# Moving one small matmul ahead of head 0's running sums in TensorE's queue

## The reference

```python
def second_block(x, ...):
    h = rms_norm(x, norm1_g)
    proj = h @ w_in
    q, k, v, glu_a, glu_b = jnp.split(proj, splits, axis=-1)
    q = rms_norm(q.reshape(bsz, seq, 8, 64), q_norm_g)     # per head
    k = rms_norm(k.reshape(bsz, seq, 8, 64), k_norm_g)
    attn = stick_breaking_attention(q, k, v)
    c = glu_a * jax.nn.sigmoid(glu_b)
    c = causal_depthwise_conv(c, conv_dw_w, conv_dw_b)     # 31 taps
    c = jax.nn.silu(layer_norm(c, conv_ln_g, conv_ln_b))
    x = x + jnp.concatenate([attn, c], axis=-1) @ w_out
    ...
# in stick_breaking_attention, per head, s < t:
#   z = q_t.k_s / sqrt(64)
#   weights = exp(log_sigmoid(z) + sum over s<j<t of log_sigmoid(-z_tj))
#   out = weights @ v
```

## Time and profile before

| what | value |
|---|---|
| three timed runs | 1307.55, 1308.39, 1308.89 us; median 1308.39 |
| the profiled execution's own time | 1306.23 us |
| its span, first to last instruction | 1304.5 us |
| mean granted TensorE clock | 0.986 of full |
| busy: TensorE, VectorE, ScalarE, GpSimd | 1258.5, 635.6, 485.4, 530.0 us |

### The profile page before, as it was taken

How to read it: one execution, slowest core, us unless ns; L and a number is a source line. 1 busy time by engine, 2 the same in 40 slices (tenths; PEclk the granted TensorE clock), 3 DMA queues, 4 the chain that set the end, 5 groups by cost and what they waited for, 6 DMA issues and landing times.

```text
span 1304.5 us, 16116 instructions
## 1 busy us (share of the span) xinstructions
PE 1258.5 (96%) x5574; PEld 1018.4 (78%) x5574; DVE 635.6 (49%) x882; ACT 485.4 (37%) x630; POOL 530.0 (41%) x244
## 2 busy tenths in 40 slices
PE   6899999999999999999979999799999999999999
PEld 6786888778888888888867776457888888888887
DVE  6829363353654155415585857694733313331332
ACT  6432342233443144314452234555533323332331
POOL 5854254223445344534454433000544353435343
PEclk9999999999999999999998999899999999999999
DMA  8432232112323222222232221000322232223222
GB/s 298 162 121 73 65 114 81 52 51 92 97 96 103 91 96 96 98 96 88 73 97 85 93 97 53 29 1 1 114 97 96 81 113 97 96 81 113 93 73 77
DMA packets 33313, 118.40 MB, mean 91 GB/s; under 512 B 3824, under 2 KB 3952, under 8 KB 32880
## 3 DMA queue, kind: packets, MB, share of 16 engines
q1 hardware_dynamic: 33120, 117.49, 27.1%
q10 hardware_dynamic: 144, 0.24, 0.1%
HBM read 115.61 MB, written 2.10 MB: 90 GB/s over the span
## 4 chain that ended last, share of the span: by engine, by line
PE 90%; DVE 6%; ACT 2%; issue 1%; DMA 0%; SPq 0%; DVEq 0%; ACTq 0%
PE ps L1028 25%; PE ps L1030 25%; PE ps L1029 25%; PE ps L1280 2%; DVE squares L625 2%; PE ps L1065 2%; PE ps L1066 2%; PE ps L1067 2%; PE ps L1263 1%; PE ps L1138 1%; PE ps L1160 1%; DVE slab L774 1%; DVE xg_lo L629 1%; PE ps L1307 1%; PE ps L1323 1%
## 5 line engine op out<-in xcount | busy, mean ns | idle before, releaser
L311 POOL TENSOR_TENSOR w_lo<-w_raw,w_hi 128x1024 fp32r<-128x1024 f32 x215 | 519.7, 2421 | 746.2 <-ACT w_hi L389 388.9
L1028 PE MATMUL ps<-xg_hi,w_hi 128*128 128x512 f32 x960 | 380.8, 397 | 10.4 <-DVE xg_lo L629 5.2
L1030 PE MATMUL ps<-xg_hi,w_lo 128*128 128x512 f32 x960 | 375.9, 392 | 0.0
L1029 PE MATMUL ps<-xg_lo,w_hi 128*128 128x512 f32 x960 | 375.7, 391 | 0.0
L1028 PE MATMUL ps<-y_hi,w_hi 128*128 128x512 f32 (+1 forms) x608 | 234.3, 385 | 13.6 <-DVE y_lo L629 10.8
L1030 PE MATMUL ps<-y_hi,w_lo 128*128 128x512 f32 (+1 forms) x608 | 231.5, 381 | 0.0
L1029 PE MATMUL ps<-y_lo,w_hi 128*128 128x512 f32 (+1 forms) x608 | 231.5, 381 | 0.0
L1028 PEld LDWEIGHTS ps<-xg_hi,w_hi 128*128 128x128 f32 x960 | 181.7, 189 | 51.4 <-DVE xg_lo L629 6.0
L1029 PEld LDWEIGHTS ps<-xg_lo,w_hi 128*128 128x128 f32 x960 | 181.8, 189 | 39.1 <-issue 1.7
L1030 PEld LDWEIGHTS ps<-xg_hi,w_lo 128*128 128x128 f32 x960 | 181.5, 189 | 38.3
L389 ACT ACTIVATE w_hi<-w_raw 128x1024 fp32r<-128x1024 f32 x136 | 143.1, 1052 | 160.3 <-PE ps L1030 126.5
(11 more groups left out here) (173 smaller groups left out, 1049.3 us busy)
## 6 DMA issues: line engine op xcount, KB each, us to landing
w_raw<-weights SPq DMA_DIRECT2D x200, 512.0 KB, 3.3
w_raw<-weights SPq DMA_DIRECT2D x16, 384.0 KB, 2.9
h<-x_t SPq DMA_DIRECT2D x2, 1024.0 KB, 11.7
out_t<-h SPq DMA_DIRECT2D x8, 256.0 KB, 2.0
slab<-mem_t SPq DMA_DIRECT2D x2, 512.0 KB, 6.1
slab<-mats_in SPq DMA_DIRECT2D x1, 1024.0 KB, 14.5
cols<-cols_in ACTq DMA_DIRECT2D x1, 231.0 KB, 4.3
corr<-corr_in SPq DMA_DIRECT2D x1, 32.0 KB, 14.4
```

Of the source, the lines that this page charges most:

```text
L311: nc.gpsimd.tensor_tensor(w_lo[:, s, :], w_raw[:, s, :], w_hi[:, s, :].bitcast(F32), ALU.subtract).then_inc(w_lo_ready, 1)
L1028: pe.matmul(out, w[0], x[0], start=first, stop=False)
L1029: pe.matmul(out, w[0], x[1], start=False, stop=False)
L1030: return pe.matmul(out, w[1], x[0], start=False, stop=last)
```

## The change

`qk_sum(7)`, TensorE's matmul for the sum of squares of the last query/key block, is put in front of `s_cumulate(0)` and was behind it. It keeps its wait on `qk_square`. Nothing else changes; the other engines' lists are the same.

```diff
                 else:
                     pe.wait_ge(s_att, 2 * 6 + 1)
                     output2(0, (0, 1), begin=True)
-                s_cumulate(hd)
                 if hd == 0:
                     qk_sum(7)
+                s_cumulate(hd)
                 if hd % 2 == 0 and hd >= 2:
                     pair_values(hd // 2 - 1)
```

## The result

The changed kernel takes 1298.34 us (median of six runs, 1294.99 to 1300.96) against 1307.42 for the kernel before (six runs); the ratio is 0.9931, with a 95% interval of 0.9914 to 0.9947. That is 9.1 us between the medians, where 8.3 were forecast; the time lies in the forecast's range. Two later sets on other occasions gave 0.9946 (0.9931 to 0.9961) and 0.9932 (0.9914 to 0.9950). The profiled execution took 1297.77 us with a span of 1296.0, 8.5 less than the span in the earlier trace rows.

What follows compares the result with a forecast made beforehand. TensorE, with 90% of the chain, was taken as the bound, time being winnable only where it idles or runs at lower clock; 5.05 + 3.29 gave 8.34 us off the median 1308.39, predicting 1300.1, range 1297.5 to 1303.6.

Steps and rivals of the forecast that it cites:

- Part 3: Behind TensorE's long gap: a short gap keeps the clock up, saving 3.29 us; one short low stretch of 1.51 us stays.
- Part 1: TensorE's block 7 sum starts 5.05 us earlier, inside the idle 1.30 us, without delaying head 0's running sums.
- rival (d): Late squares block TensorE ahead of head 0's running sums: slower, 1311.0 us if they come at 826.8; chance 0.02.
- Part 2: ScalarE's run behind block 7's sum, and so head 2's scores on TensorE, start 5.05 us earlier.
- The term of 3.29 us: From head 2's scores to head 3's: 7.62 us at full clock in place of 10.91.
- The term of 1.51: Loss in the second, shorter low-clock stretch at head 5's scores, 0.41 + 1.10 us; the forecast keeps one such stretch.
- rival (a): Full clock throughout the stage: 9.85 us saved, 1298.5 us; chance 0.25.
- rival (b): Only the moved run counts; head 2's scores and head 1's sums stay at low clock: 5.05 us saved, 1303.3; chance 0.2.
- Part 4: VectorE loses its slack up to the last convolution tap: half a microsecond left at full clock, 2.0 us with 8.34 saved.
- (c): The move is eaten by two more short low-clock stretches in later gaps: 2.0 us saved, 1306.4 us; chance 0.04.

Runs made afterwards that it cites:

- both orders: Kernel before with block 7's sum moved as in the change, and ScalarE and VectorE taking block 7's root after head 1's softplus: 1297.55 us, ratio 0.9918.
- the filled kernel: Changed kernel plus 7 and 5 unread 128x512 matmuls in TensorE's gaps behind head 0's and head 1's running sums: 1294.89 us, ratio 0.9901.

## Why the prediction was right

The forecast came true, in the time and in the mechanism of its first two parts; that the number came so close is in part luck, as Part 3 shows.

**Part 1 held.** The squares were long there, the matmul moved by 5.05 us relative to head 1's scores, as forecast, and fits the idle slot, and the running sums did not move. The rival (d), a wait ahead of the squares, did appear one step further on: 0.82 us in the kernel with the sum ahead of head 1's scores. It did not make that kernel slower: ScalarE took the root of block 7's sum beside head 1's scores and no longer ahead of the softplus, and head 2's scores still came 0.79 us earlier.

**Part 2 held, and it is the cause of the first 5 us.** Head 2's scores came 5.00 us earlier (5.05 forecast). Two places of the matmul give one for one. With the release taken back only 0.88 remain; with ScalarE's order changed and TensorE's left alone the gap goes as well. Reading ScalarE's bank beside TensorE's sums cost nothing: 1.24 us on the chain before and after.

**Part 3 had the mechanism right and its size per execution not to be had from one trace.** The term of 3.29 us was worth 1.12, 1.13 and 3.29 us in the three traces of the changed kernel. The term of 1.51 (1.63 by the pieces, since the scores taken as full clock still had 0.11 us of the low clock in them), which the forecast left at nothing, was won in the first and third and not in the second. The stage took 51.17, 52.83 and 48.88 us; forecast were 50.6 with one short stretch and 49.1 at full clock. So rival (a) occurred in the third. The first came near the forecast by another way: the low stretch stood under head 2's scores and head 1's sums, where the forecast had none, and not at head 5's, where it had kept one; 5.00 + 1.12 + 1.63 make up for 5.05 + 3.29. With the 0.73 us won ahead of the stage, the profiled execution took 1297.77 us against the 1297.9 forecast for it, and that closeness is luck. The second, with both stretches, lies nearer to rival (b)'s 53.9 than to the forecast's 50.6. The median of 9.1 us lies between 8.34 and 9.85.

The forecast's reading of which gap brings the clock down was too definite. A gap of 1.65 us was followed by a fall in two traces and by none in the third; one of 1.07 ahead of head 5's scores by a fall in three traces (before, the changed kernel's second, both orders) and by none in the others where it was left idle; one of 1.30 ahead of 128-row matmuls by a fall in the trace of ScalarE's order alone, though the prediction had read 1.52 us ahead of such matmuls as harmless. That idle time counts is shown best by the kernel before with its long gap filled: head 3's scores 8.12 us behind head 2's where it was 10.91, and an interval clear of no change. In the three traces of kernels with fillers in their short gaps the clock did not fall in this stage either, but nor did it in two traces without (the third of the changed kernel, and the one with the sum ahead of head 1's scores); there the evidence is the times of the runs, and the interval of the filled kernel (0.9886 to 0.9916) still touches that of the changed one (0.9914 to 0.9947). The Trainium skill (TensorE: Matmul & The Clock Gate, "What's actually happening") says that the monitor behind the clock runs on its own and is not reset by a kernel's start, so that the same kernel shows different numbers of slow matmuls. The three traces of the changed kernel agree in that one program lost 2.17, 2.16 and 0 us between head 2's and head 3's scores; the monitor itself no trace here shows.

**Part 4 held.** VectorE was put at 0.5 us of slack at full clock; adding 2.18 us of load gave 1.81 us of wait, so it was about 0.3. In the changed kernel's first trace the last tap ends at 866.47 and the channel sums start at 866.75. The forecast had 2.0 us of slack at such a gain, from a low stretch at head 5; the stretch came earlier, VectorE waited along with it (0.89 and 1.57 us ahead of two softplus steps), and the slack was 0.28. In the second trace, with a stretch at head 5, it was 1.88. The estimate that the stage can't give much over 10 us holds for the changed order; with both orders, whose taps start earlier, the channel sums come 11.4 us earlier (47.47 against 58.91), and there VectorE closes up.

**The rivals.** (b), only the moved run counts, would have been 5.05 us; two of the three traces of the changed kernel had its low stretch, but for 2.17 of the 3.29 us; (c) did not occur, nor did (d) in the changed kernel.

What stays open is why the kernel with the release taken back gained 2.9 us where its shift is 0.88. Its clock levels were 0.980 to 0.987 against 0.980 to 0.987 of the kernel before, and its one trace had a stage 3.01 us shorter, by clock for the greater part. More traces of both would tell whether the fill of the 1.3 us slot lowers the chance of a low stretch.

## What to carry to other kernels

In an engine that works strictly in order, a small operation costs what stands behind it in the queue of whoever waits for it: look for the short producer whose consumer's queue holds something long that another engine needs, and move either of the two. Read the clock of the stretch behind every gap of TensorE; where it falls, closing the gap can pay twice, and a gap that can't be closed may be filled with matmuls that nobody reads. One profile shows one draw of the clock, so a stage is best compared in pieces between fixed starts, each with its clock beside it.

## What the runs showed of the hardware

Twenty useless 128x512 matmuls in an idle gap of TensorE made the kernel 4.4 us faster by the ratio (2.4 to 6.4): no work was released earlier, and the granted clock behind the gap was higher. Gaps as short as 1.07 us, ahead of matmuls with 64 rows, were followed by stretches at 0.50 that cost 1.6 to 3.3 us; one of 1.30 us ahead of matmuls with 128 rows was followed by one that cost 1.6. The same gaps were also followed by none. The six runs of the changed kernel in one set scatter by 6.5 us with the clock (1295.23 at 0.992, 1301.71 at 0.984). With two of its gaps filled four runs scatter by 0.7 us, and five runs by 3.4 with VectorE loaded besides; the twelve runs with only the long gap filled scatter by 8.3.
